# Moving the product with V and the probabilities' transposes ahead of the projection products in each attention unit of a hybrid block kernel

## The chip, the cores and the metric

The kernel runs on one core of one Trainium2 chip. The metric is device time in microseconds (us) for one execution, as the median of several runs. The engines are TensorE (PE in the profile; PEld is its weight loads), VectorE (DVE), ScalarE (ACT), GpSimd (POOL) and SyncE (SP), which issues most of the transfers.

## The reference, cut to what matters

One layer over 1024 positions with 1024 features: a combined input projection, a short gated convolution beside a banded attention of 8 heads of 64, an output projection with a residual, and a two-layer MLP with a squared ReLU. The change lies in the first part, where the projection is computed beside the attention.

```python
xn = rms_norm(x, norm_mix_g[l])
z = jnp.einsum("bsd,dc->bsc", xn, w_in[l])     # columns [B | C | h | q | k | v]
y_conv = short_gated_conv(gb, gc, hh, conv_w[l], conv_b[l])
y_attn = chunk_band_attention(q, k, v, q_norm_g[l], k_norm_g[l], rel_bias[l])
y_mix = concat([group_rms_norm(y_conv, ...), group_rms_norm(y_attn, ...)])
x = x + einsum("bsc,cd->bsd", y_mix, w_out[l])
hid = square(relu(einsum(rms_norm(x, norm_mlp_g[l]), w_mlp_in[l])))
x = x + einsum("bsf,fd->bsd", hid, w_mlp_out[l])
```

In the attention each chunk of 64 queries sees its own and the 8 chunks before it: scores with a relative bias, a softmax, and the product with V.

## The kernel before, in words

**Numbers.** Every fp32 matrix operand is held as two parts of type fp32r, a rounded high part and the low rest; a product is three matmuls (high by high, high by low, low by high: `PASSES`).

**Stages.** A first stage normalises and transposes the input. The second, which the change touches, is four iterations (`iteration(it, last)`), one for each pair of heads; three run in a hardware loop and the fourth is written out as `last`. The output projection and the MLP follow.

**An iteration** has 16 units (`UNITS`): 8 tiles of 128 queries times two heads. Unit u has `keys(u)` key blocks of 128, 1 for the first two units, rising to 5 from unit 8 on. Its attention work goes round between the engines:

- PE `score(it, u)` (lines 1664 and 1665) writes the scores to the PSUM tile SC;
- DVE `scores` (1191) adds the bias and finds the maximum (the semaphore `sm_done`);
- ACT `exps` (766) takes the exponentials (`exp_done`);
- PE `prob_transpose` (1675) transposes the probabilities into PT, one 128x128 transpose for each key block;
- ACT `pt_hi` (772) and DVE `pt_lo` (1198) copy them to SBUF as high and low part (`pthi_done`, `ptlo_done`);
- PE `prob_v` (1688) multiplies them with V, one matmul of 256 columns for each key block; it waits for `ptlo_done` of its unit;
- DVE `u_sum` (1206) adds the two halves (`us_done`), PE `u_transpose` (1695) turns the result back, and DVE `o_sum` (1214) adds again, once for two units.

**The fill.** Between these PE does the projection products of the same and the next pair of heads: `fill(count)` issues the next `count` matmuls of 512 columns of a running list (line 1628). 24 of them are one group (one kind and one half of the positions); the last raises `proj_done`, for which ACT, DVE and POOL wait. `FILL` gives 14 products to each of the first 8 units and 15 to the others, `FILL_LAST` 14 to each of the first 12 units, then 12, 12, 0 and 0. Each unit's count is split into `count // 2` and the rest.

**The other work.** `extras(f"{u}a")` and `extras(f"{u}b")` place further steps at a unit: on PE the sums of squares (1641, 1642), the transposes of v (1728) and of the attention output (`o_transpose`, 1701); on DVE the norms and the convolution. DVE's own order in unit u is `scores(u + 1)`, `u_sum(u - 1)`, extras a, `pt_lo(u)`, extras b. In unit 3 extras a are `squares_lo` (1101) and the two halves of `inverse` (1112, 1115); in unit 13 the two last convolution taps (`conv_tap`, 1154 and 1158), which come after tap 1150 of unit 12. ACT's order is `exps(u + 1)`, `pt_hi(u)`, then its steps for that unit, `deviation` (724, 726, 728) and `o_store` (783) among them. POOL makes the low and high part of the projection weights, one cast (529) and two subtractions (532) for each kind of column, when `proj_done` says that the slot's last reader is through.

**Order.** Each engine runs its list in the order written; nothing but semaphores ties them together. PE's order in unit u before the change is: u_transpose(u-2), score(u+1), the first half of the fill, extras a, prob_v(u-1), prob_transpose(u), the rest of the fill, extras b. After unit 15 an iteration goes on with the rest of its projection products (runs of 2, 8, 13, 15 and 18).

Of the kernel before, what the change touches and what calls it, by code (L numbers as in the profile page):

```python
# [56 lines left out]
def build(nc, x, norm_mix_g, w_in, conv_w, conv_b, q_norm_g, k_norm_g, rel_bias,  # L57
          conv_out_g, attn_out_g, w_out, norm_mlp_g, w_mlp_in, w_mlp_out, out):
    ctx = ExitStack()
    with ctx:  # L60
# [609 lines left out]
        def _(act):  # L670
# [128 lines left out]
            def ym_hi(t):  # L799
                act.activation(ym(t, HI), ymix[:, t], ACT.Copy).then_inc(s["ymhi_done"], 1)  # L800
# [6 lines left out]
            def iteration(it, last):  # L807
                exps(it, 0)
                for u in range(UNITS):
                    if u + 1 < UNITS:  # L810
                        exps(it, u + 1)
                    pt_hi(it, u)
                    if u == 0:
                        take(it, 2)
                    if u == 2:
                        take(it, 3)
                        deviation(it, 2)
                    if u == 3:
                        v_copy(it, 1)
                    if u == 4:  # L820
                        qk_hi(it, 2)
                        deviation(it, 3)
                    if u == 5:
                        v_hi(it, 1)
                        c_copy(it, 0)
                        qk_hi(it, 3)
                    if u == 9:
                        act.wait_ge(s["y_done"], it * 2 + 1)
                        squares(it, 4, zs[:, 2])
                    if u == 10:  # L830
                        o_dev(it, 0)
                        c_copy(it, 1)
                        deviation(it, 4)
                    if u == 12:
                        o_store(it, 0)
                    if u in (11, 12) and last:

                        act.wait_ge(s["proj_done"], PRIMED + (NPAIR - 1) * G + u - 1)
                        wo_hi(u - 11)
                    if u == 12 and last:  # L840
                        act.wait_ge(s["w_ready"], N_B)
                        act.wait_ge(s["ss_read"], it * 8 + (OTURN[0] + 3))
                        act.wait_ge(s["znc_done"], it * 2 + 1)
                        ym_hi(0)
                    if u == 13 and last:
                        act.wait_ge(s["proj_done"], PRIMED + NPAIR * G)
                        act.activation(vT[:, :], PJ[:, (G - 1) % 2], ACT.Copy).then_inc(s["b_copied"], 1)
                    if u == 13 and not last:
                        act.wait_ge(s["y_done"], it * 2 + 2)
                        squares(it, 5, zs[:, 2])  # L850
                    if u == 14 and not last:
                        take(it + 1, 0)
                        deviation(it, 5)
                    if u == 14 and last:
                        ym_hi(1)
                        wo_hi(2)
# [731 lines left out]
        def _(pe):  # L1588
# [142 lines left out]
            def iteration(it, last):  # L1731
                n = 0

                def fill(count):
                    nonlocal n
                    for m in range(n, n + count):
                        g = NLEAD + m // (3 * KD)
                        group_product(it + g // G, g % G, m % (3 * KD))
                    n += count

                def extras(at):
                    if at == "2a":
                        sum_squares(it, 2)
                    if at == "4a":
                        sum_squares(it, 3)
                    if at == "4b":
                        v_transpose(it, 1)
                    if at == "10b":
                        sum_squares(it, 4)
                    if at == "12a":  # L1750
                        o_transpose(it, 0, OTURN[0])
                    if at == "14b" and not last:
                        sum_squares(it, 5)
                    if at == "15b" and not last:
                        sum_squares(it + 1, 0)
                    if last:
                        if at == "14b":
                            u_transpose(it, UNITS - 3)
                            w_out_both(0, (0,))
                        if at == "15b":  # L1760
                            w_out_both(1, (0,))
                            w_out_both(0, (1,))
# [3 lines left out]
                for u in range(UNITS):  # L1766
                    count = (FILL_LAST if last else FILL)[u] - (4 if u == 0 else 0)
                    if u >= 2 and not (last and u == UNITS - 1):
                        u_transpose(it, u - 2)
                    if u + 1 < UNITS:  # L1770
                        score(it, u + 1)
                    fill(count // 2)
                    extras(f"{u}a")
                    if u >= 1:
                        prob_v(it, u - 1)
                    prob_transpose(it, u)
                    fill(count - count // 2)
                    extras(f"{u}b")
                if not last:
# [193 lines left out]
```

## Time and profile before

| | |
|---|---|
| median of 3 runs | 1110.6 us (1109.13 to 1110.92) |
| the profiled execution's own time | 1111.08 us |
| its span, first to last instruction | 1109.3 us |
| PE busy | 1099.6 us, 99% of the span |
| DVE, ACT, POOL busy | 718.3, 543.1, 621.2 us |
| granted TensorE clock, mean | 1.000 |
| projection products (line 1628, 512 columns) | x1128, 290.6 us |
| product with V (line 1688) | x240, 40.1 us |
| transposes of probabilities (line 1675) | x240, 36.6 us |

Matmuls are pipelined: a matmul's length in the profile contains a tail in which the next has already started. What a run of matmuls costs is read from the start of the run to the start of the next thing, not from its length. The page divides the span into 40 slices of 27.7 us; the four iterations lie in slices 2 to 15.

### The profile page before, as it was taken

Reading aid. Unit: us, or ns where it says so; the run is one execution under the profiler, and the core shown is the slowest. Engines: PE = TensorE matmul, PEld = TensorE weight load, DVE = VectorE, ACT = ScalarE, POOL = GpSimd, SP = SyncE. Lnnn points to the kernel's source line nnn. Section 1 sums busy time; section 2 is a strip of 40 time slices with the busy share of each in tenths; the row PEclk is TensorE's granted clock in tenths of the full one; section 3 lists DMA queues with packets and bytes.
Section 4 is the critical chain, followed back from the end, with each engine's and each line's share of the span. In section 5 each row is a group of like instructions: output and inputs, shape, how many; then the busy total and the mean of one; then the engine's idle time right before and its main releaser. Section 6 shows DMA issues by size and latency. Waiting matters only on the chain.

```text
span 1109.3 us, 14646 instructions
## 1 busy us (share of the span) xinstructions
PE 1099.6 (99%) x5248; PEld 915.7 (83%) x5248; DVE 718.3 (65%) x907; ACT 543.1 (49%) x890; POOL 621.2 (56%) x363
## 2 busy tenths in 40 slices
PE   9999999999999999999999999999999999999998
PEld 7888888888888888887888888888888888888886
DVE  7577757767766786465443443434568785877798
ACT  7664664565466564345445545454453244333330
POOL 4313131240412040148888787878789796896992
PEclk9999999999999999999999999999999999999999
DMA  8311110110110415122564545444785446345324
GB/s 247 100 37 39 42 57 19 45 52 19 57 36 23 152 58 190 58 76 67 168 202 140 164 142 162 152 155 158 257 289 194 134 160 221 118 150 190 101 76 171
DMA packets 98369, 135.27 MB, mean 122 GB/s; under 512 B 8057, under 2 KB 52097, under 8 KB 98314
## 3 DMA queue, kind: packets, MB, share of 16 engines
q1 hardware_dynamic: 94960, 130.60, 35.1%
q10 hardware_dynamic: 3354, 3.94, 1.2%
q8 instruction: 34, 0.56, 0.2%
q14 instruction: 21, 0.17, 0.0%
HBM read 96.75 MB, written 39.34 MB: 123 GB/s over the span
## 4 chain that ended last, share of the span: by engine, by line
PE 95%; DVE 2%; ACT 1%; issue 1%; DMA 0%; ACTq 0%; DVEq 0%
PE PJ L1628 23%; PE SC L1894 10%; PE PJ L1894 10%; PE OS L1894 8%; PE PT L1931 7%; PE SC L1931 7%; PE OS L1931 7%; PE PJ L1931 7%; PE PJ L1706 6%; PE OS L1688 3%; PE PT L1675 2%; PE SC L1664 1%; PE SC L1665 1%; PE OS L1695 1%; PE PT L1628 1%
## 5 line engine op out<-in xcount | busy, mean ns | idle before, releaser
L1628 PE MATMUL PJ<-actT,wsl 128*128 128x512 f32 x1128 | 290.6, 399 | 0.1
L1628 PEld LDWEIGHTS PJ<-actT,wsl 128*128 128x128 f32 x1128 | 202.5, 188 | 38.0 <-DVE actT L1080 0.5
L641 POOL TENSOR_TENSOR ring<-b,ring 128x1024 fp32r<-128x1024 f32 x48 | 139.2, 2910 | 37.2 <-ACT ring L1020 37.1
L1517 DVE TENSOR_TENSOR ring<-hraw,ring 128x1024 fp32r<-128x1024 f32 x56 | 148.3, 2682 | 5.6 <-ACT ring L1015 5.6
L529 POOL CAST wsl<-raw 128x1024 fp32r<-128x1024 f32 x23 | 25.4, 1103 | 186.2 <-PE PJ L1628 162.7
L1015 ACT ACTIVATE ring<-hraw 128x1024 fp32r<-128x1024 f32 x56 | 59.2, 1057 | 133.3 <-PE OS L1931 59.9
L1894 PE MATMUL OS<-actT,w1a 128*128 128x512 f32 x384 | 92.4, 390 | 0.8 <-ACT p1s L947 0.8
L766 ACT ACTIVATE prob<-prob,negm 128x640 f32<-128x640 f32 (+4 forms) x64 | 44.4, 693 | 90.0 <-DVE negm L1191 89.9
L1894 PEld LDWEIGHTS OS<-actT,w1a 128*128 128x128 f32 x384 | 71.9, 188 | 16.0 <-issue 1.2
L1931 PE MATMUL PT<-ring 128*128 128x512 f32 x336 | 80.8, 389 | 0.1
L1931 PE MATMUL OS<-ring 128*128 128x512 f32 x336 | 80.7, 389 | 0.0
L1931 PE MATMUL PJ<-ring 128*128 128x512 f32 x336 | 80.6, 389 | 0.0
L1931 PE MATMUL SC<-ring 128*128 128x512 f32 x336 | 80.6, 389 | 0.0
L1931 PEld LDWEIGHTS PT<-ring 128*128 128x128 f32 x336 | 63.0, 188 | 13.6 <-issue 0.5
L1931 PEld LDWEIGHTS OS<-ring 128*128 128x128 f32 x336 | 63.1, 188 | 13.1
L1931 PEld LDWEIGHTS SC<-ring 128*128 128x128 f32 x336 | 63.1, 188 | 13.1
L1931 PEld LDWEIGHTS PJ<-ring 128*128 128x128 f32 x336 | 63.1, 188 | 13.1
L570 POOL TENSOR_TENSOR w1a<-w1r,w1a 128x512 fp32r<-128x512 f32 x32 | 51.4, 1605 | 30.7 <-ACT w1a L941 30.7
L1706 PE MATMUL PJ<-wo,actT 128*128 128x512 f32 x288 | 67.5, 392 | 0.3 <-DVE h L1454 0.3
L532 POOL TENSOR_TENSOR wsl<-raw,wsl 128x512 fp32r<-128x512 f32 x46 | 64.7, 1428 | 1.8
L565 POOL TENSOR_TENSOR wsum<-w1r 128x512 f32<-128x512 f32 x32 | 41.8, 1306 | 39.9 <-DVE ymix L1462 39.9
L1206 DVE TENSOR_REDUCE uT<-OS 128x128 f32<-128x256 f32 x64 | 27.1, 424 | 56.3 <-PE OS L1688 56.2
(221 smaller groups left out, 2239.2 us busy)
## 6 DMA issues: line engine op xcount, KB each, us to landing
hraw<-hidd SPq DMA_DIRECT2D x56, 512.0 KB, 3.7
w1r<-in_w_mlp_in SPq DMA_DIRECT2D x16, 1024.0 KB, 6.2
hidd<-hs SPq DMA_DIRECT2D x64, 256.0 KB, 2.0
b<-in_w_mlp_out SPq DMA_DIRECT2D x16, 1024.0 KB, 7.6
raw<-in_w_in SPq DMA_DIRECT2D x24, 512.0 KB, 3.8
hidd<-h SPq DMA_DIRECT2D x48, 256.0 KB, 2.3
xin<-in_x SPq DMA_DIRECT2D x8, 512.0 KB, 6.7
woraw<-in_w_out SPq DMA_DIRECT2D x8, 512.0 KB, 7.1
```

What stands on the lines that cost most here:

```text
L532: op = nc.gpsimd.tensor_tensor(wsl[:, sl, LO, k], raw_k[:, w % 2, k], wsl[:, sl, HI, k].bitcast(F32), ALU.subtract)
L565: nc.gpsimd.tensor_tensor(wsum[:, j], x0, x1, op).then_inc(s["st_done"], 1)
L570: nc.gpsimd.tensor_tensor(w1_slot(name, LO), w1_operand(name, i), w1_slot(name, HI).bitcast(F32), ALU.subtract).then_inc(s["w1lo_done"], 1)
L641: nc.gpsimd.tensor_tensor(duo(n)[1][LO], W2_SRC[name][:, 2 * d:2 * d + 2], duo(n)[1][HI].bitcast(F32), ALU.subtract).then_inc(s["wl2_done" ...
L766: act.activation(prob[:, u % 2, 0:L], prob[:, u % 2, 0:L], ACT.Exp, bias=negm[:, u:u + 1], scale=-1.0, accum_out=esum[:, u:u + 1]).then_in ...
L1015: act.activation(duo(n)[0][HI], hraw[:, n % HRING], ACT.Copy).then_inc(s["hh2_done"], 1)
L1517: vec.tensor_tensor(duo(n)[0][LO], hraw[:, n % HRING], duo(n)[0][HI].bitcast(F32), ALU.subtract).then_inc(s["hl2_done"], 1)
L1628: last = mm(PJ[:, g % 2, cols] if out_ is None else out_[:, cols], wsl[:, w % NSLOT, a, k], actT[:, b, k, c], start=(r == 0), stop=(r == 3 ...
L1688: last = mm(UP, V[:, t - nb + 1 + j, hh].rearrange("p a d -> p (a d)"), pT[:, :, j * P:(j + 1) * P], start=(j == 0), stop=(j == nb - 1))
L1706: last = mm(SC[:, half(hf)] if t == 1 else PJ[:, hf], ym(t, a)[:, k], wo[:, k, b, half(hf)], start=(k == 0 and n == 0), stop=(k == KD - 1 ...
L1894: last = mm(out_, w1_slot(name, a)[:, k], moving(name, b, k), start=(r == 0 and name in ("P1", "P6", "P7")), stop=(r == 11), skip_group_ch ...
L1931: last = mm(out_, hid_[a][:, j, p * P:(p + 1) * P], w_[b][:, j, :], start=(r == 0 and d == 0 and name in ("P1", "P6", "P7")), stop=(r == 5 ...
```

## The change

In each unit but the first, PE now does prob_v(u-1) and prob_transpose(u) right after score(u+1), and then the whole fill; extras a stand in the middle of it, where the two halves meet. Unit 0 keeps its order. With the extras, o_transpose(it, 0) moves from 12a to 12b in the three loop iterations, and ACT's o_store(it, 0), which reads what it writes, from unit 12 to unit 13. In the last iteration these two keep their names of place.

```diff
@@ ScalarE, iteration
-                    if u == 12:
+                    if u == (12 if last else 13):
                         o_store(it, 0)
@@ TensorE, extras
-                    if at == "12a":
+                    if at == ("12a" if last else "12b"):
                         o_transpose(it, 0, OTURN[0])
@@ TensorE, iteration
                     if u + 1 < UNITS:
                         score(it, u + 1)
-                    fill(count // 2)
-                    extras(f"{u}a")
-                    if u >= 1:
+                    if u == 0:
+                        fill(count // 2)
+                    else:
                         prob_v(it, u - 1)
                     prob_transpose(it, u)
+                    if u:
+                        fill(count // 2)
+                    extras(f"{u}a")
                     fill(count - count // 2)
                     extras(f"{u}b")
```

No instruction is added or taken away, apart from register instructions of the sequencers. DVE's and POOL's lists are the same.

PE in unit 14 of a loop iteration, before (uT is the operand of u_transpose, SC<-kT and SC<-kL are the scores, PJ<-actT,wsl the projection products, OS<-pT,V the product with V, PT<-ident,prob the transposes of the probabilities):

```order
L1695 MATMUL OS<-ident,uT 128x128
L1658 REGISTER_ALU
L1664 MATMUL SC<-kT,qz 128x384
L1665 MATMUL SC<-kL,qz 128x384
L1664 MATMUL SC<-kT,qz 128x256
L1665 MATMUL SC<-kL,qz 128x256
L1628 MATMUL PJ<-actT,wsl 128x512 x7
L1688 MATMUL OS<-pT,V 128x256 x5
L1675 MATMUL PT<-ident,prob 128x128 x5
```

and after:

```order
L1695 MATMUL OS<-ident,uT 128x128
L1658 REGISTER_ALU
L1664 MATMUL SC<-kT,qz 128x384
L1665 MATMUL SC<-kL,qz 128x384
L1664 MATMUL SC<-kT,qz 128x256
L1665 MATMUL SC<-kL,qz 128x256
L1688 MATMUL OS<-pT,V 128x256 x5
L1675 MATMUL PT<-ident,prob 128x128 x5
L1628 MATMUL PJ<-actT,wsl 128x512 x14
```

The product with V of unit 13 comes seven projection products earlier after the scores; these seven stand behind the transposes of unit 14, in one run with the rest.

PE in unit 4 of a loop iteration, before (OS<-sqh,ones and OS<-sql,ones are a sum of squares, extra 4a):

```order
L1665 MATMUL SC<-kL,qz 128x384
L1628 MATMUL PJ<-actT,wsl 128x512 x7
L1639 REGISTER_ALU
L1640 REGISTER_ALU
L1641 MATMUL OS<-sqh,ones 128x512
L1642 MATMUL OS<-sql,ones 128x512
L1688 MATMUL OS<-pT,V 128x256 x2
L1675 MATMUL PT<-ident,prob 128x128 x3
```

and after:

```order
L1665 MATMUL SC<-kL,qz 128x384
L1688 MATMUL OS<-pT,V 128x256 x2
L1675 MATMUL PT<-ident,prob 128x128 x3
L1628 MATMUL PJ<-actT,wsl 128x512 x7
L1639 REGISTER_ALU
L1640 REGISTER_ALU
L1641 MATMUL OS<-sqh,ones 128x512
L1642 MATMUL OS<-sql,ones 128x512
```

The product with V of unit 3 follows the scores of unit 5 at once, ahead of seven projection products and of the sum of squares.

ACT around units 12 and 13 of a loop iteration, as a difference (L766 are the exponentials, L772 is pt_hi, L783 o_store, L704 and L705 the squares of the convolution's output):

```order
+L765 REGISTER_ALU
+L766 ACTIVATE prob,esum<-prob,negm 128x640
+L772 ACTIVATE pT<-PT 128x640
 L783 ISA
 L783 ACTIVATE ymix<-OS,prm 128x4x128
-L765 REGISTER_ALU
-L766 ACTIVATE prob,esum<-prob,negm 128x640
-L772 ACTIVATE pT<-PT 128x640
 L704 ACTIVATE sq<-zs 128x512
```

The store of the first half's attention output now stands behind the exponentials of unit 14 and the copy of unit 13, ahead of the squares.

## Rows read from the trace of the kernel before

**Rows 1.** The page: each engine's busy share, and the granted TensorE clock per slice.
```profile
PE 1099.6 (99%) x5248; PEld 915.7 (83%) x5248; DVE 718.3 (65%) x907; ACT 543.1 (49%) x890; POOL 621.2 (56%) x363
...
PEclk9999999999999999999999999999999999999999
```

**Rows 2.** The waits of PE: waiting line, releaser; total us, times, longest us.
```profile
PE OS L1688 <- DVE pT L1198: 0.4, 2, 0.2
```

**Rows 3.** PE timeline, one unit, second iteration: start us, us, operation, count.
```profile
184.07 1.78 PE L1628 MATMUL PJ<-actT,wsl 128*128 128x512 f32 x7
185.69 0.76 PE L1688 MATMUL OS<-pT,V 128*128 128x256 f32 x5
186.28 0.71 PE L1675 MATMUL PT<-ident,prob 128*128 128x128 f32 x5
186.75 2.09 PE L1628 MATMUL PJ<-actT,wsl 128*128 128x512 f32 x8
188.68 0.40 PE L1641 MATMUL OS<-sqh,ones 128*128 128x512 f32 x1
```

**Rows 4.** PE timeline, end of that iteration: longer runs of projection products.
```profile
219.67 3.24 PE L1628 MATMUL PJ<-actT,wsl 128*128 128x512 f32 x13
222.75 0.40 PE L1641 MATMUL OS<-sqh,ones 128*128 128x512 f32 x1
...
223.22 3.58 PE L1628 MATMUL PJ<-actT,wsl 128*128 128x512 f32 x15
226.63 0.60 PE L1728 MATMUL PT<-ident,vT 128*128 128x128 f32 x4
```

**Rows 5.** Timeline, POOL, DVE and PE, around unit 13's split, second iteration.
```profile
202.35 1.04 POOL L529 CAST wsl<-raw 128x1024 fp32r<-128x1024 f32 x1 [4.83 <-PE PJ L1628]
...
203.47 2.99 POOL L532 TENSOR_TENSOR wsl<-raw,wsl 128x512 fp32r<-128x512 f32 x2
...
203.62 1.69 DVE L1154 SCALAR_TENSOR_TENSOR zs<-ub,prm,zs 128x512 f32<-128x512 f32 x1
...
205.34 1.67 DVE L1158 SCALAR_TENSOR_TENSOR zs<-ub,prm,zs 128x512 f32<-128x512 f32 x1
...
206.17 1.78 PE L1628 MATMUL PJ<-actT,wsl 128*128 128x512 f32 x7
...
207.04 0.82 DVE L1198 TENSOR_TENSOR pT<-PT,pT 128x640 fp32r<-128x640 f32 x1
...
207.92 0.87 PE L1688 MATMUL OS<-pT,V 128*128 128x256 f32 x5
...
208.62 0.49 PE L1675 MATMUL PT<-ident,prob 128*128 128x128 f32 x3
```

**Rows 6.** DVE timeline: a convolution tap while POOL is idle.
```profile
173.74 0.75 DVE L1154 SCALAR_TENSOR_TENSOR zs<-ub,prm,zs 128x512 f32<-128x512 f32 x1
```

**Rows 7.** Timeline, units 2 and 3, second iteration, all engines.
```profile
150.44 0.56 DVE L1191 CUSTOM_DVE_ANT_0 prob<-SC,bias 128x384 f32<-128x384 f32 x1
...
151.34 0.63 ACT L728 ACTIVATE rt<-sq 128x512 f32<-128x512 f32 x1
...
151.81 1.04 POOL L529 CAST wsl<-raw 128x1024 fp32r<-128x1024 f32 x1 [3.48 <-PE PJ L1628]
...
152.15 0.42 DVE L1206 TENSOR_REDUCE uT<-OS 128x128 f32<-128x256 f32 x1 [1.14 <-PE OS L1688]
...
152.49 0.91 DVE L1101 TENSOR_TENSOR sql<-sq,sqh 128x512 fp32r<-128x512 f32 x1
...
154.03 1.06 DVE L1115 SCALAR_TENSOR_TENSOR sq<-rt,sq 128x512 f32<-128x512 f32 x1
...
154.23 1.78 PE L1628 MATMUL PJ<-actT,wsl 128*128 128x512 f32 x7
...
155.02 0.41 DVE L1198 TENSOR_TENSOR pT<-PT,pT 128x256 fp32r<-128x256 f32 x1
```

**Rows 8.** PE timeline, last iteration: the product with V of unit 14.
```profile
396.12 0.86 PE L1688 MATMUL OS<-pT,V 128*128 128x256 f32 x5 [0.18 <-DVE pT L1198]
```

## Prediction, on record before the changed kernel was timed

> **What bounds the kernel now.** I read the page first. PE is busy 99% of the span and its granted clock is full in all slices, while DVE, ACT and POOL are at 65, 49 and 56% [rows 1]. So only two things can move the time: PE waiting less or more, and PE's own spacing of the same instructions. The second view is the list of PE's waits: for the step that the change moves it holds one entry, the product with V waiting for DVE's low part, 0.4 us in all [rows 2]. It counts only time in which no matmul was left running, so a short stall shows better in the starts. The third is PE's timeline over one unit, to see what a run costs from start to start [rows 3, 4]. The fourth is the timeline of all engines at the places where the moved product has least room [rows 5 to 7].
>
> **What the change does to each engine.** PE has the same 5248 matmuls. In units 1 to 15 of three iterations and 1 to 13 of the last, 58 in all, two runs of projection products become one (the last iteration has none in units 14 and 15). With 5 key blocks the product with V takes 0.59 us and the transposes 0.47 us, start to start [rows 3]. Both move forward by the first half of the fill, 7 products or 1.62 us; the first half moves back by 1.06 us, and the second half stays where it was. The instruction queues of DVE, POOL and SP are unchanged. In ACT's queue only the store of the attention output passes another step.
>
> **Term 1, the wait at unit 13's split.** Before, the two convolution taps of unit 13 run on DVE at 203.62 and 205.34 and take 1.69 and 1.67 us, while POOL makes weights from 202.35 to 206.46 [rows 5]. The same tap takes 0.75 us with POOL idle [rows 6]. Behind them pt_lo ends at 207.86, and the product with V starts at 207.92, 1.75 us after its fill began, where an undisturbed fill takes 1.62 us. It then takes 0.70 us instead of 0.59 us. The stall costs 0.13 + 0.11 = 0.24 us in each of the three loop iterations.
>
> After the change this product is wanted at 206.17. DVE's u_sum ahead of the taps waits for a product that also comes 1.62 us earlier, but DVE first has its scores, so I put the taps' start at 202.4 rather than 202.0. POOL is released by a projection product in the first half of the fill, 1.06 us later: cast from 203.41. So both taps, 0.75 us each, are through at 203.9 with hardly any overlap, and pt_lo, 0.82 us, at 204.7. That is 1.4 us ahead of the need. The wait goes: 3 x 0.24 = **0.7 us less**.
>
> The last iteration's waits give nothing. There pv of unit 14 waits 0.18 us [rows 8] on exponentials of unit 15, whose scores come no earlier. What unit 13 gains is waited off there.
>
> **Term 2, one run for two.** A run of 7 costs 1.62 us, 0.231 each; 8 behind transposes cost 1.93 us [rows 3]. Thirteen behind transposes cost 3.08 us and fifteen behind a 512-column matmul 3.41 us, 0.227 each [rows 4]. So a run seems to need some products to settle, and merging saves one settling. Five products added to the run of 8 cost 3.08 - 1.93 = 1.15 us, 0.230 each. Seven more at 0.227 to 0.230 cost 1.59 to 1.61 us, against 1.62: 0.01 to 0.03 us for each unit. I take 0.02 x 58 = **1.2 us less**. The ends are 0 and (0.231 - 0.227) x 15 x 58 = 3.5 us, if all fifteen ran at the settled pace. I stay near the lower one, since the run of 13 is the nearest case, also behind transposes.
>
> [...]
>
> **Term 3, the seam.** pv's first matmul now follows a score matmul of 256 columns instead of one of 512. Its weight load must fit behind the shorter one. Five matmuls of 256 columns in a row take 0.59 us, each with its own load [rows 3], so the load fits at that width. I cost this at nothing. If it did not, up to 0.05 us for each of 58 units would be 2.9 us; a gain here has no mechanism.
>
> **Term 4, a new wait in unit 4.** The product of unit 3 has 2 key blocks and three DVE steps ahead of its pt_lo. It is now wanted where the fill starts, 154.23; before, pt_lo ended at 155.43 [rows 7]. DVE's work by the new order: scores to 151.00; u_sum 0.42 us without its idle 1.14 us, to 151.42; squares_lo and the first half of inverse, at most 0.75 us each like a tap alone, to 152.9. (ACT's last step of the deviation ends at 151.97 even if nothing moves it.) The second half of inverse reads two SBUF tiles. POOL's cast, 151.81 before, starts 0.45 us later, since two matmuls of V and two transposes now stand ahead of its release, and ends at 153.3. Before, squares_lo met the same cast and ended at 153.40, 0.55 us after it. So inverse ends near 153.9 and pt_lo, which overlapped its forerunner by 0.07 us and takes 0.41, at 154.2. That is just at the need and too late for the weight load ahead of it. The price of being late just so is up to the 0.24 us of term 1; I take 0.08 x 4 = **0.3 us more**. Lower end 0; upper end, if DVE did not move forward at all, 155.43 - 154.23 = 1.2 us, 4.8 us in four iterations.
>
> **The rest at nothing.** Unit 5 has the same pattern with more room, as have all others where I followed DVE this way. The exponentials for prob_transpose are a whole unit old. u_transpose and the next scores gain room, as DVE's steps for them come no later. o_transpose has some 8 projection products less room after it, but the next user of its bank is two units on. o_store, on a half-idle ACT, stands ahead of squares that wait for DVE's convolution; without that cover it would cost its own length of some 0.7 us on ACT, not on PE. POOL's weights are made at most 1.06 us later; their readers are two groups, 48 products, away. SP's loads follow them.
>
> **Sum.** 1111.1 - 0.7 - 1.2 + 0.3 = 1109.5 us against the profiled execution, which lies 0.5 us over the median. Against the median of 1110.6 us it is **1109.0 us**.
>
> **The rivals.**
> (a) *Merging gives nothing.* Terms 1 and 4 alone: 1110.6 - 0.4 = 1110.2 us. For it: the difference is a few ns in 230. Against: the longer runs of rows 4.
> (b) *Merging gives the settled pace.* Term 2 near 3 us: 1107.2 us. For it: the run of 15 at 0.227. Against: it does not stand behind transposes.
> (c) *A wait on DVE takes the place of the one removed.* One mechanism: pt_lo of unit 3 ends late because DVE's steps and POOL's cast still meet as before, so that the product with V waits where before seven fill products and a sum of squares covered it. Between nothing and 1.2 us in each iteration; it makes the kernel slower on balance from 0.5 us an iteration on. At 1.2 us: 1110.6 - 0.7 - 1.2 + 4.8 = 1113.5 us. For it: room was only a few tenths in my walk. Against: DVE idles 1.14 us there before, which the change gives back.
> (d) *The seam costs.* The change is made, but each unit pays 0.05 us: 1109.0 + 2.9 = 1111.9 us.
> (e) *The clock falls.* Narrow work now stands together: transpose, scores, V, transposes, then 15 wide products. At half clock the 1.06 us of V and transposes would take twice that, 58 x 1.06 = 61 us more, 1170 us. Against it: the clock is full in every slice although narrow and wide work alternate already [rows 1, 3]. The Trainium skill (TensorE: Matmul & The Clock Gate, Part 4: PE-mode transpose) says that transposes do not count as activity for the clock as matmuls do; by that rule longer narrow stretches are a danger, and the trace so far shows no effect.
> (f) *It does not do what it says*: PE could be held by something else right after the scores, such as the semaphores of V and transposes now asked for together. That would look like (d).
>
> **How the numbers follow.** A measurement of this kernel can tell about 0.2%, 2.2 us, from no change. My forecast, 1107.9 to 1110.1 us, has 0.48; (a) 0.17; (b) 0.20; (c) 0.08; (d) with (f) 0.06; (e) 0.01. Faster by over 0.2%, below 1108.4 us: all of (b) and a quarter of the forecast, 0.33. Slower by over 0.2%, above 1112.8 us: most of (c), (e) and a part of (d), 0.10. The rest, 0.57, is within 0.2%. The range from 1107.0 to 1111.9 us takes in the forecast, (a), and most of (b) and (d).
>
> **What would show it.** Right: the entry of PE waiting for DVE at line 1688 shrinks to the last iteration's part; the taps of unit 13 fall to about 0.75 us each; a fill of 15 takes 3.50 to 3.54 us from start to start, and the unit of rows 3 about 0.02 us less in sum. Wrong: pt_lo of unit 3 ends over 0.3 us after the scores of unit 5; the first matmul with V starts over 0.13 us after the last of the scores in undisturbed units; a granted clock below full.

## The result, and the profile after

The changed kernel takes **1117.28 us** (median of 6 runs, 1116.71 to 1119.79) beside 1110.45 us before (6 runs, 1109.13 to 1111.70, on the same chip). The ratio is 1.0067, 95% interval [1.0057, 1.0078]: slower, by about 7 us. The prediction said 1109.0 us, in a range from 1107.0 to 1111.9. It was wrong in sign and outside its range. The profiled execution took 1118.59 us, with a span of 1116.8 us against the 1109.3 us of before.

The page answers to [rows 1]. PE's busy time grew with the span, its clock is full, and nothing else stands out. The busy share stays at 99%, although the iterations below hold over 10 us of stalls:

```profile
PE 1105.3 (99%) x5248; PEld 917.5 (82%) x5248; DVE 717.1 (64%) x907; ACT 540.1 (48%) x890; POOL 617.6 (55%) x363
...
PEclk9999999999999999999999999999999999999999
```

The waits of PE in the kernel after (waiting line, releaser; total us, times, longest us) answer to [rows 2]. The entry that I had forecast to shrink went from 0.4 to 0.3 us. That says nothing of unit 13 in the loop: both of its waits before, at 392.84 and 396.12 us, were in the last iteration. Another entry, for the same line of PE, stands above it, and its releaser is `o_sum`, a DVE step that the prediction does not mention:

```profile
PE OS L1688 <- DVE on L1214: 2.6, 7, 0.6
...
PE OS L1688 <- DVE pT L1198: 0.3, 1, 0.3
```

The view of that one DVE line, in the kernel after, says who waited for it. Before, the same view names nobody.

```profile
L1214 DVE TENSOR_REDUCE on<-OS x32: 416/423/425, 56.5 to 412.7; 128x128 f32<-128x256 f32 x32
...
  PEld OS L1688: 2.9, 6
  PE OS L1688: 2.6, 7
```

**The wait in a usual unit.** PE's and DVE's timeline in unit 5 of the second iteration, kernel after (start us, us, engine, line, operation, count, idle before and its releaser):

```profile
162.12 0.27 PE L1695 MATMUL OS<-ident,uT 128*128 128x128 f32 x1
...
162.15 0.47 PE L1664 MATMUL SC<-kT,qz 128*128 128x512 f32 x1
...
162.43 0.42 DVE L1214 TENSOR_REDUCE on<-OS 128x128 f32<-128x256 f32 x1 [1.79 <-PE OS L1695]
162.46 0.40 PE L1665 MATMUL SC<-kL,qz 128*128 128x512 f32 x1
...
162.91 0.62 PE L1688 MATMUL OS<-pT,V 128*128 128x256 f32 x3
...
163.37 0.49 PE L1675 MATMUL PT<-ident,prob 128*128 128x128 f32 x3
```

The code says why. `prob_v(it, u)` for even u from 2 on waits not only for its own pt_lo but also for `oq_done`, DVE's `o_sum` of the pair of units before. That `o_sum` waits for the `u_transpose` with which the odd unit begins. The product's result and the transposed sums are two halves of one PSUM tile (`UP` and `UQ` in OB), so this wait is what keeps the product behind DVE's reading of the sums. Before the change, seven fill products, 1.62 us, stood between `u_transpose` and the product [rows 3]. Now only the scores do, and the round trip from PE to DVE and back is on PE's path: from 162.12 to 162.91, **0.79 us**, of which the reduction itself is 0.42. In the kernel before, DVE's reduction also comes 0.3 us behind the transpose, and PE never notices, since the product stands 2.2 us behind it (timeline, kernel before, the same unit):

```profile
158.93 0.27 PE L1695 MATMUL OS<-ident,uT 128*128 128x128 f32 x1
...
159.24 0.42 DVE L1214 TENSOR_REDUCE on<-OS 128x128 f32<-128x256 f32 x1 [0.95 <-PE OS L1695]
...
159.50 1.78 PE L1628 MATMUL PJ<-actT,wsl 128*128 128x512 f32 x7
...
161.12 0.52 PE L1688 MATMUL OS<-pT,V 128*128 128x256 f32 x3
...
161.47 0.49 PE L1675 MATMUL PT<-ident,prob 128*128 128x128 f32 x3
```

How I price a stall: the last score matmul starts at 162.46, and the next matmul should start 0.23 us later, at 162.69. It starts at 162.91: 0.22 us. The three products then take 0.46 us to the first transpose, where before they took 0.35 (161.12 to 161.47): 0.11 us more. So this unit stalls 0.32 us with rounding, although the list of waits counts almost nothing here, since the last score matmul was still running.

**The worst unit.** In unit 15 there are no scores to issue (there is no unit 16), and the product stands directly behind the transpose, kernel after:

```profile
215.51 0.28 PE L1695 MATMUL OS<-ident,uT 128*128 128x128 f32 x1
...
215.82 0.42 DVE L1214 TENSOR_REDUCE on<-OS 128x128 f32<-128x256 f32 x1 [1.76 <-PE OS L1695]
...
216.39 0.83 PE L1688 MATMUL OS<-pT,V 128*128 128x256 f32 x5 [0.61 <-DVE on L1214]
...
217.06 0.49 PE L1675 MATMUL PT<-ident,prob 128*128 128x128 f32 x3
```

Here the round trip is 0.88 us and the stall 0.85.

**The whole account.** I went through all 64 products with V in this way. By product of unit, an iteration of the loop now stalls 0.43 (unit 2), 0.32 (4), 0.20 (6), 0.26 (8), 0.26 (10), 0.26 (12) and 0.85 us (14), and nothing at the odd ones: about 2.57 us together, where it was 0.25 us, all at unit 13. The last iteration stalls 2.83 us, where it was 0.92; 0.92 us of that is still at its units 13 and 14, where the product waits for pt_lo. That sums to 10.53 us after and 1.66 before, **+8.9 us**. The four iterations, from the first score to a matmul of the output projection that has the same place in both lists (411.01 us before, 419.56 after), take 375.24 us after and 367.55 before, **+7.7 us**. The difference, 1.2 us, is what the change gave elsewhere. It is known to some 0.3 us, since it hangs on what is called the usual distance of an undisturbed product. PE's later stages agree within 0.02 us each. What varies is the start of the program, ahead of the first score, between 42.3 and 44.4 us over all the profiles of this study, and the stretch from the last matmul to the end, 3.6 to 3.7 us in some and 4.5 to 4.8 in the others. That is why the iterations alone are a sharper measure than the spans.

**The places that I had predicted.** The fill in unit 9 is one run of 15 between transposes and the next `u_transpose`, kernel after:

```profile
183.69 3.69 PE L1628 MATMUL PJ<-actT,wsl 128*128 128x512 f32 x15
187.22 0.28 PE L1695 MATMUL OS<-ident,uT 128*128 128x128 f32 x1
```

It takes 3.53 us from start to start, against 1.62 + 1.93 = 3.55 us in two runs [rows 3]. The convolution taps of unit 13 (DVE timeline, kernel after) no longer meet POOL, and pt_lo is through long before its product:

```profile
206.37 0.74 DVE L1154 SCALAR_TENSOR_TENSOR zs<-ub,prm,zs 128x512 f32<-128x512 f32 x1
207.15 0.75 DVE L1158 SCALAR_TENSOR_TENSOR zs<-ub,prm,zs 128x512 f32<-128x512 f32 x1
207.93 0.82 DVE L1198 TENSOR_TENSOR pT<-PT,pT 128x640 fp32r<-128x640 f32 x1
```

They took 1.69 and 1.67 us before [rows 5]. And in unit 4 pt_lo ends 1.0 us before the product that needs it starts:

```profile
156.03 0.42 DVE L1198 TENSOR_TENSOR pT<-PT,pT 128x256 fp32r<-128x256 f32 x1
...
157.46 0.40 PE L1688 MATMUL OS<-pT,V 128*128 128x256 f32 x2
```

### The profile page after: what moved, and what is told of

Same layout as the page of the kernel before. It is cut to its first block, busy times and chain, and to the rows that moved or that the text cites. A ratio compares the mean times of both kernels' runs of the same rounds, so it can differ in the third digit from the quotient of the medians.

```text
span 1116.8 us, 14646 instructions
## 1 busy us (share of the span) xinstructions
PE 1105.3 (99%) x5248; PEld 917.5 (82%) x5248; DVE 717.1 (64%) x907; ACT 540.1 (48%) x890; POOL 617.6 (55%) x363
## 4 chain that ended last, share of the span: by engine, by line
PE 95%; DVE 3%; ACT 1%; issue 1%; DMA 0%; ACTq 0%; DVEq 0%
PE PJ L1628 23%; PE SC L1897 10%; PE PJ L1897 10%; PE OS L1897 8%; PE PT L1934 7%; PE SC L1934 7%; PE PJ L1934 7%; PE OS L1934 7%; PE PJ L1706 6%; PE OS L1688 3%; PE PT L1675 2%; PE SC L1664 1%; PE SC L1665 1%; PE OS L1695 1%; PE PT L1628 1%
## 5 line engine op out<-in xcount | busy, mean ns | idle before, releaser
L1628 PE MATMUL PJ<-actT,wsl 128*128 128x512 f32 x1128 | 281.2, 398 | 0.1
L1628 PEld LDWEIGHTS PJ<-actT,wsl 128*128 128x128 f32 x1128 | 205.4, 188 | 40.9 <-DVE actT L1080 0.6
L766 ACT ACTIVATE prob<-prob,negm 128x640 f32<-128x640 f32 (+4 forms) x64 | 44.6, 697 | 115.3 <-DVE negm L1191 115.1
L1191 DVE CUSTOM_DVE_ANT_0 prob<-SC,bias 128x640 f32<-128x640 f32 (+4 forms) x64 | 42.0, 656 | 38.2 <-PE SC L1665 37.5
L1706 PEld LDWEIGHTS PJ<-wo,actT 128*128 128x128 f32 x288 | 53.5, 188 | 11.5 <-issue 0.7
```

Of the source, the lines that this page charges most:

```text
L766: act.activation(prob[:, u % 2, 0:L], prob[:, u % 2, 0:L], ACT.Exp, bias=negm[:, u:u + 1], scale=-1.0, accum_out=esum[:, u:u + 1]).then_in ...
L1191: vec.tensor_tensor_reduce(out=prob[:, u % 2, 0:L], in0=SC[:, c0:c0 + L], in1=bias[:, u % 2, BANDW - L:BANDW], scale=-1.0, scalar=3.0e38, ...
L1628: last = mm(PJ[:, g % 2, cols] if out_ is None else out_[:, cols], wsl[:, w % NSLOT, a, k], actT[:, b, k, c], start=(r == 0), stop=(r == 3 ...
L1706: last = mm(SC[:, half(hf)] if t == 1 else PJ[:, hf], ym(t, a)[:, k], wo[:, k, b, half(hf)], start=(k == 0 and n == 0), stop=(k == KD - 1 ...
```

## The experiments

**Theory A**: what costs is the round trip `u_transpose`, DVE's `o_sum`, product with V, which only odd units have, and which the scores alone don't cover. **The rival**: something spread over all units, such as the seam between scores and product or the narrow work standing together. All kernels were timed beside the kernel before (medians 1110.13 to 1110.17 us). They differ from it and from the change only in the order of instructions.

### 1. The new order in half of the units

```diff
-                    if u == 0:
+                    early = u >= 1 and u % 2 == 0
+                    if not early:
                         fill(count // 2)
-                    else:
+                        extras(f"{u}a")
+                    if u >= 1:
                         prob_v(it, u - 1)
                     prob_transpose(it, u)
-                    if u:
+                    if early:
                         fill(count // 2)
-                    extras(f"{u}a")
+                        extras(f"{u}a")
```

The second kernel has `early = u % 2 == 1`, the third `early = u >= 1 and u != 15`.

Even units alone:

> The new order only in even units (where the product with V is of an odd unit and does not wait for DVE's o_sum); odd units keep the old order. Theory A (in odd units the product with V of an even unit waits for o_sum, which waits for the u_transpose issued just ahead, and only the scores cover that round trip): no stall at any product with V, unit 13's stall gone too, half of the merging gain: 1110.5 - 0.7 - 0.8, about 1109. Rival B (each product with V that follows the scores directly pays, by the sequencer or a late low part): about half of the loss stays, 1110.5 + 3.4, about 1114.

Measured: 1124.65 us, ratio 1.0131 [1.0115, 1.0146]. A miss by 16 us, the slowest kernel of the study. The wait list of this kernel shows what took over, and the timeline of its unit 4 how (scores, DVE's pt_lo of unit 3, and the product of unit 3):

```profile
PE OS L1688 <- DVE pT L1198: 11.9, 13, 1.6
```

```profile
157.73 0.34 PE L1665 MATMUL SC<-kL,qz 128*128 128x384 f32 x1
...
158.68 0.41 DVE L1198 TENSOR_TENSOR pT<-PT,pT 128x256 fp32r<-128x256 f32 x1
159.14 0.30 PEld L1688 LDWEIGHTS OS<-pT,V 128*128 128x128 f32 x2 [1.39 <-DVE pT L1198]
159.14 0.51 PE L1688 MATMUL OS<-pT,V 128*128 128x256 f32 x2 [1.07 <-DVE pT L1198]
```

The product of an odd unit is now early, while the transposes of that unit, in the old order, are late. So the path from the transposes over ACT and DVE to the product is shorter than a unit, and the product waits 1.34 us (unit 3), 0.83 (5), 0.22 (11) and 1.85 us (13) in each iteration of the loop. The first half of the expectation held all the same: no product of an even unit stalls (at most 0.01 us in the loop), since it stands behind the fill as before. What I had missed is that the change moves two things that depend on each other, and that moving both keeps their distance while moving one does not. As a test of Theory A this run is therefore poor by its time, and good only by where the stalls are.

Odd units alone:

> The new order only in odd units. Theory A: all of the new waits, 2.6 us in each of three iterations and about 2 in the last, less half of the merging gain, unit 13's old stall kept: 1110.5 + 9.5 - 0.8, about 1119, slower than the change itself. Rival B: half of the loss, about 1114.

Measured: 1119.80 us, ratio 1.0092 [1.0077, 1.0108]. The stalls are at the products of even units, 0.43, 0.32, 0.38, 0.26, 0.26, 0.57 and 0.85 us, 3.07 us an iteration. The odd units alone carry all of the loss of the change, and a little more.

Unit 15 as before:

> The change, with unit 15 alone in the old order. Unit 15 has no scores of a next unit, so nothing at all covers the wait for o_sum. Theory A: its stall of 0.85 us goes in each of the three loop iterations: 1117.3 - 2.5, about 1114.8. Rival B: unit 15 is one of 15, the gain is about 0.5 us: 1116.8.

Measured: 1115.91 us, ratio 1.0051 [1.0038, 1.0065]. The stall of 0.85 us is gone from every iteration of the loop, the others stay (1.75 us an iteration), and an iteration is 0.76, 0.70 and 0.79 us shorter than with the change. So one of the seven stalls is priced by itself. The median came out 1.1 us higher than expected; I have no cause for that, within the 2.2 us that a measurement can tell.

### 2. Fill products between the round trip's ends

These keep the new order and put one or two products of the unit's first half ahead of the product with V, in odd units alone:

```diff
-                    if u == 0:
-                        fill(count // 2)
-                    else:
+                    lead = (count // 2 if u == 0 else 1 if u % 2 and count else 0)
+                    fill(lead)
+                    if u:
                         prob_v(it, u - 1)
                     prob_transpose(it, u)
                     if u:
-                        fill(count // 2)
+                        fill(count // 2 - lead)
```

One product:

> The same with one product, 0.23 us. Theory A: each stall shrinks by 0.23 us or to nothing: unit 3 to 0.20, unit 5 to 0.09, units 7 to 13 to about 0.03 or less, unit 15 to 0.62; in all 1117.3 - 6.0, about 1111.3. A theory in which the wait is for something that moves with the product itself would leave the stalls at their length.

Measured: 1112.34 us, ratio 1.0019 [1.001, 1.0028]. The stalls: 0.20 us at unit 2, 0.09 at unit 4, 0.00 at unit 6, 0.03 at units 8, 10 and 12, 0.69 at unit 14. That is what one product of 0.23 us should leave, but for 0.07 us more at unit 14; the product of unit 3 now stalls 0.10 us, on pt_lo. The median is 1.0 us over the 1111.3 expected. In unit 15 (PE and DVE timeline of this kernel) the round trip is still 0.88 us, with one product now inside it:

```profile
211.00 0.27 PE L1695 MATMUL OS<-ident,uT 128*128 128x128 f32 x1
...
211.31 0.42 DVE L1214 TENSOR_REDUCE on<-OS 128x128 f32<-128x256 f32 x1 [1.77 <-PE OS L1695]
...
211.88 0.82 PE L1688 MATMUL OS<-pT,V 128*128 128x256 f32 x5 [0.37 <-DVE on L1214]
```

Two products:

> The change, with two of the fill's products left between the scores and the product with V in odd units. Theory A (a round trip through DVE's o_sum of fixed length, covered only by what PE does behind u_transpose): two products cover 0.46 us more, so the stalls of units 3 to 13 (0.2 to 0.43 us) go, and unit 15's 0.85 us falls to about 0.4: 1117.3 - 8.3, about 1109. Rival B (the time is lost by the joint of narrow matmuls itself): no better than the change by more than 1 us.

Measured: 1111.09 us, ratio 1.0004 [0.9995, 1.0013]. All stalls of usual units are gone; unit 14's product still waits 0.38 us. This is 6 us faster than the change, but 2 us above what I expected. The stalls at the product with V sum to 2.65 us, so the rest sat elsewhere: PE's wait list for this kernel shows 1.4 us at the scores, where the change has 0.3, and the timeline at the start of the second iteration shows why (DVE, POOL, PE):

```profile
PE SC L1664 <- DVE negm L1191: 1.4, 3, 0.8
```

```profile
137.12 2.27 DVE L1130 TENSOR_TENSOR kL<-zs,kT 64x512 fp32r<-64x512 f32 x2
```

```profile
137.80 1.04 POOL L529 CAST wsl<-raw 128x1024 fp32r<-128x1024 f32 x1 [9.07 <-PE PJ L1628]
```

```profile
140.37 0.33 PE L1664 MATMUL SC<-kT,qz 128*128 128x128 f32 x1 [0.78 <-DVE negm L1191]
```

DVE's two subtractions for kL take 0.69 us each, at most, in every other profile of this study. Here POOL's cast starts at 137.80, just before the second of them would (137.12 + 0.70 = 137.82). The cast takes 1.04 us, as when it is alone, and DVE's second subtraction 1.56 us. In the kernel with two and four products (below) it is the other way round, DVE first and POOL longer:

```profile
135.91 1.40 DVE L1130 TENSOR_TENSOR kL<-zs,kT 64x512 fp32r<-64x512 f32 x2
```

```profile
136.64 1.56 POOL L529 CAST wsl<-raw 128x1024 fp32r<-128x1024 f32 x1 [9.10 <-PE PJ L1628]
```

There the cast starts 0.73 us behind kL, here 0.68, with the first subtraction's 0.70 between. I take this for chance between two engines; one profile of each can't show more, and it is argued, not shown. The other part of the excess was in the first iteration, where DVE waited 0.53 us for a bias that a transfer brought late.

### 3. The sum turned back earlier

Here `u_transpose(u - 1)` is issued inside unit u, after half of the fill (first kernel) or three products before its end (second), instead of at the start of unit u + 1. Nothing but distance changes for the round trip.

```diff
-                    if u >= 2 and not (last and u == UNITS - 1):
-                        u_transpose(it, u - 2)
...
                     if u:
                         fill(count // 2)
+                    if u and not (last and u > UNITS - 3):
+                        u_transpose(it, u - 1)
                     extras(f"{u}a")
                     fill(count - count // 2)
...
                     fill(rest - 54)
-                    u_transpose(it, UNITS - 2)
```

In the middle of the fill:

> The change, with u_transpose(u-1) issued in the middle of unit u's fill in place of u_transpose(u-1) at the start of unit u+1; every wait is kept. Theory A: DVE's o_sum is through long before the product with V asks for it, so all stalls at line 1688 go, and unit 13's with them: 1117.3 - 9.5, about 1107.8, under both kernels; the run of 15 is split by one 128-column transpose, which may give back up to 1 us of the merging gain. Rival B: the seam stays as it is, about 1117.

Measured: 1111.14 us, ratio 1.0007 [0.9998, 1.0016].

Three products before its end:

> The change, with u_transpose(u-1) three products ahead of the end of unit u's fill instead of in its middle. Cover for o_sum is three products and the scores, about 1.2 us, against a round trip of about 1 us, so the stalls at the product with V stay away as in the kernel with it in the middle. What this tells apart: if a run of projection products needs some ten products to settle, a run of 12 keeps most of what merging gives, and the time is 1.0 to 1.5 us under the kernel with the transpose in the middle (1111.1): about 1109.8. If the merging gain was not real, the two are equal.

Measured: 1109.98 us, ratio 0.9996 [0.9987, 1.0005].

In both the stalls at the product with V fall to 1.04 and 1.07 us, below the kernel before: Theory A is right about them. But the gain of the merged run did not come. The profile of the first one, PE's timeline in unit 9 of the second iteration:

```profile
185.04 1.87 PE L1628 MATMUL PJ<-actT,wsl 128*128 128x512 f32 x7
186.75 0.27 PE L1695 MATMUL OS<-ident,uT 128*128 128x128 f32 x1
186.77 2.09 PE L1628 MATMUL PJ<-actT,wsl 128*128 128x512 f32 x8
188.70 0.39 PE L1641 MATMUL OS<-sqh,ones 128*128 128x512 f32 x1
```

From 185.04 to 188.70 are 3.66 us. The transpose's own 0.11 us taken off, the fill takes 3.55 us, just what the two runs took before, against 3.53 in one run. One transpose of 128 columns in the run undoes the merging. I had expected 1107.8 us of the first kernel, some 3 us too few; the merging's 1.2 us explains a part of that, and the rest is open. Of the second I had expected 1109.8 us, if a run of 12 keeps most of the gain. The median of 1109.98 us meets that by luck: the two kernels' iterations agree in their profiles (367.58 and 367.47 us), so the 1.2 us between their medians is not explained by the order, and the run of 12 kept next to nothing.

### 4. The move of the store and of one transpose alone

The diff of the change also moves `o_store` and `o_transpose` by half a unit. This kernel is the one before with those two edits only.

> The kernel before, with only o_transpose at 12b and the output's store in unit 13. Both theories: no change, 1110.1 us; a part of the loss here would be against both.

Measured: 1110.29 us, ratio 0.9999 [0.999, 1.0008]. No difference.

### 5. A version that keeps the gain without the wait

As the kernel with two products, with four in unit 15:

```diff
-                    lead = (count // 2 if u == 0 else 2 if u % 2 and count else 0)
+                    lead = (count // 2 if u == 0 else 4 if u == UNITS - 1 and count else 2 if u % 2 and count else 0)
```

> The changed order, with two of the unit's fill products ahead of the product with V in odd units and four in unit 15 of the iterations that have fill there; even units as in the change. Theory A (what costs is the round trip from PE's transpose of the sum to VectorE's reduction of it and back, 0.79 us, 0.88 in unit 15): two products and the scores (0.5 + 0.45 us) cover it, four cover it in unit 15, so the stalls at the product with V come to about 0.1 us per iteration, and the joined run keeps its gain: a region of some 93.6 us against 94.1 before, 1108.8 us, faster than both kernels. In the run with two products in every odd unit, two iterations lost 0.6 to 0.9 us more at their start: there POOL's cast started between the two halves of VectorE's kL (2.27 us for the pair in place of 1.40), and the scores of unit 1 waited 0.78 us. If that arrival falls the same way again here, 1110.0. Rival: the gain of the joined run does not outlast a split, and the time is that of before, 1110.

Measured: **1108.98 us**, ratio 0.9986 [0.9977, 0.9995] to the kernel before: the only version whose interval lies below 1, by little. Of the waits of the product with V, its wait list keeps only the one in the last iteration, which has no fill left to put there:

```profile
PE OS L1688 <- DVE pT L1198: 0.4, 1, 0.4
```

The stalls are 0.11, 0.12, 0.13 and 1.14 us in the four iterations, 1.50 in all, and the iterations take 366.46 us, 1.09 less than before. The cast did not come ahead of kL's second half here, as its rows above show.

The same with the column sums one product earlier in the tail of the iteration (`fill(12)` and `fill(16)` in place of 13 and 15), to give kL more distance from POOL's cast, and the control, that edit alone on the kernel before:

> The same, and the column sums of squares for the next iteration are put one product earlier in the tail of the iteration (12 and 16 products around them in place of 13 and 15). They release the chain ScalarE, VectorE that ends in kL; POOL's cast hangs on a projection product and stays. If the wait at the iteration's start is the arrival of POOL's cast between kL's two halves (margin 0.03 us in the profiled run), kL now starts 0.2 us earlier against the cast, its second half is under way when the cast comes, and no iteration shows 2.27 us for the pair or a wait at unit 1's scores: 1108.8 us or below. If the wait has another cause it stays where it was in the run without this edit.

> The kernel before, with the column sums one product earlier in the tail and nothing else. Its profile shows kL's pair at 1.40 us, so the arrival is on the good side there; expected no change, 1110.1 us within 0.2%. If it is faster, the gain of the run before this one is not the order's.

Measured: 1109.79 us, ratio 0.9994 [0.9985, 1.0003], and 1110.03 us, ratio 1.0001 [0.9992, 1.001]. Neither profile shows a long kL, but the run without the edit shows none either, so this pair confirms nothing about the cause of the wait in the run with two products. Its iterations take 366.56 us, the same as without it within 0.1 us, though its median is 0.8 us higher and can't be told from the kernel before. So medians of two kernels with equal iterations differ by up to about 1 us here, and the gain of 1.1 us rests on the iterations in both profiles more than on the medians.

### The account over all kernels

"Stalls" is the sum at the product with V over all 64, each against the usual distance of an undisturbed one, from 0.02 us on; "iterations" is the time of all four; both are from the profile. "Rest" is the difference of the iterations to before, less that of the stalls, and is known to some 0.3 us.

| kernel | median us | ratio | stalls us | iterations us | rest us |
|---|---|---|---|---|---|
| before | 1110.45 | | 1.66 | 367.55 | |
| the change | 1117.28 | 1.0067 | 10.53 | 375.24 | -1.18 |
| even units | 1124.65 | 1.0131 | 16.41 | 381.79 | -0.51 |
| odd units | 1119.80 | 1.0092 | 12.17 | 377.55 | -0.51 |
| unit 15 as before | 1115.91 | 1.0051 | 8.08 | 373.03 | -0.94 |
| one product | 1112.34 | 1.0019 | 5.18 | 369.91 | -1.16 |
| two products | 1111.09 | 1.0004 | 2.65 | 369.09 | +0.55 |
| two and four | 1108.98 | 0.9986 | 1.50 | 366.46 | -0.93 |
| two and four, column sums earlier | 1109.79 | 0.9994 | 1.47 | 366.56 | -0.80 |
| before, column sums earlier | 1110.03 | 1.0001 | 1.66 | 367.58 | +0.03 |
| sum turned in mid-fill | 1111.14 | 1.0007 | 1.04 | 367.58 | +0.65 |
| sum turned late | 1109.98 | 0.9996 | 1.07 | 367.47 | +0.51 |
| store's move alone | 1110.29 | 0.9999 | 1.67 | 367.62 | +0.06 |

The rest is about -0.8 to -1.2 us where nearly all units have one long run of fill (58 runs merged, or most of a run in half of them), about half of that where half the units do, and nothing gained where the run is cut by a transpose. The kernel with two products is the exception, by the waits at its scores.

## Why the prediction was wrong, by its own steps

**Term 1 was right**: the wait at unit 13's split went, in all three iterations of the loop, and the taps take 0.74 and 0.75 us where 0.75 was said.

**Term 2 was right**: 0.01 to 0.03 us a merged run was the estimate, 0.02 the value taken; 1.2 us over 58 runs is 0.021. A fill of 15 takes 3.53 us, within the 3.50 to 3.54 named. That the size came out so near is in part luck, as the timeline shows 0.02 us as two steps of its last digit; but the gain comes and goes with the cut through the run, as the turned-back sums in mid-fill show. The Trainium skill (TensorE: Matmul & The Clock Gate, Back-to-back issue gap) gives a matmul of 512 columns an isolated gap of N / 2.4 + 2.5, some 216 ns, and in a stream with weight loads a sustained 131 ns. This case's trace agrees with neither: in the fill of unit 9 of the change the products start, from the second on, 226 to 236 ns apart, and 226 or 227 ns from the seventh to the fourteenth.

**Term 3 was right**: nothing at the seam. The products of odd units follow 256-column scores just as closely in the new order, and stall nothing.

**Term 4 measured nothing** where I had 0.08 us in each iteration: pt_lo of unit 3 ended 1.0 us ahead of its product. That holds for the change only because the product of unit 2 had already been delayed, and POOL's cast with it, but not DVE. In all kernels where that wait is small (the sum turned back earlier, one, two and four products), DVE's second half of `inverse` meets the cast and takes 1.20 to 1.44 us instead of 0.69, and the product of unit 3 stalls 0.10 to 0.14 us, 0.4 to 0.5 us in four iterations. The estimate of 0.3 us was right in kind, and near in size, for a kernel without the wait that I had missed.

**The step that failed is "The rest at nothing"**, with its sentence that u_transpose and the next scores gain room. I followed the waits of the product with V by the entry that the profile shows, DVE's pt_lo, and in the code that is its first wait of three. The third, `oq_done` for even units, had never shown, as 1.62 us of fill covered it. The list of the kernel's steps that I worked from names only `ptlo_done` for `prob_v` too. The change takes exactly that cover away. The walk asked whether each DVE step that feeds the product could be earlier; for `o_sum` it can't, because PE itself releases it, at the start of the same unit. The price is the term that was missing, put at nothing: seven products in each iteration of the loop and six in the last, 0.20 to 0.85 us each, 9.6 us in all (the 8.9 us above with term 1's 0.7 put back). With it, and nothing for term 4, the sum would have been 1111.1 - 0.7 - 1.2 + 9.6 = 1118.8 us for the profiled execution, which was 1118.59. That is an account and not a test, as 9.6 and 1.2 are read from the same profile; the tests are the kernels above.

**Of the rivals**, (c) had the right form, a wait on DVE taking the place of the one removed, and the right sign. It named pt_lo of unit 3, one place an iteration, and so reached 1113.5 us and a chance of 0.08. (f) named the right place, PE held right after the scores by a semaphore of the moved step; it did not say which, was priced like (d), 1111.9 us, and had 0.06 together with it. Had either been followed through the three waits of `prob_v`, it would have met `oq_done`. One of the signs that I had named for a wrong forecast is there, a first matmul with V that starts over 0.13 us after the last of the scores: in units 9, 11 and 13 it starts 0.30 us after (182.26 to 182.56 in unit 9), in even units with the same scores 0.12. I had meant it for the seam. (a), (b), (d) and (e) don't fit: merging gives something and not three us, the seam costs nothing, the clock is full in every slice. The rule of the Trainium skill (TensorE: Matmul & The Clock Gate, Part 4: PE-mode transpose), that transposes do not count as activity for the clock as matmuls do, showed no effect: the granted clock is 0.999 or 1.000 in every run.

The change does not save less than I thought; it saves 1.9 us, as I thought (0.7 and 1.2), and pays 9.6 us for it at a wait that I didn't list. What stays open: whether the product could do without the wait on `o_sum`, if its result and the sums' lay in different PSUM banks. It wasn't tried: the four PSUM tiles of this kernel (PJ, SC, PT, OS) are all in use, and another place for one of the two would need further steps moved.

## What to carry to other kernels

- Before moving an instruction forward, write down every semaphore that its function waits for, also the ones that appear in no wait list, and for each the instruction that releases it and how far ahead that stands in the new order. A wait that the profile never shows is one whose cover may be what you are about to take away.
- A round trip over another engine costs its full length once nothing stands inside it (here 0.79 to 0.88 us for a reduction of 0.42). Two fill products bought it back here, four where no scores help, and moving two dependent steps together or not at all kept the other path whole.
- A stall that begins while the last matmul is still running is hardly seen in a wait list (2.6 us here of more than 9); take starts against starts.

## What the runs showed of the hardware that was not expected

- **A run of products is a little cheaper when nothing narrow cuts it.** In unit 9 fifteen products of 512 columns take 3.53 us in one run and 3.55 in runs of 7 and 8. With a single 128-column transpose between 7 and 8 of them they take 3.55 again, the transpose's own 0.11 us taken off (an estimate: four transposes take 0.43 us from start to start, 161.69 to 162.12). Over the 58 units of the change this is 1.2 us. A split of 2 and 13, with the narrow work between, in half of the units still left 0.8 to 0.9 us of it.
- **A matmul that had to wait costs more than the wait.** Behind a stall of 0.22 us the first product of 256 columns took 0.11 us longer than its 0.12 to its successor. At nearly every stall it was 0.07 to 0.11 us, and a third or more of what the short ones cost.
- **Where DVE steps with two SBUF inputs meet POOL's work, the later one pays most.** A tap of 0.75 us takes 1.69 when it starts behind POOL's subtraction [rows 5, 6] and 0.74 without it. POOL's cast takes 1.04 us when it comes first, and DVE's subtraction then 1.56 instead of 0.69; when DVE's comes first it keeps its 0.69 and the cast takes 1.56. A shift of 0.05 us between the two went with a wait of 0.78 us on PE in one run.
